# Weight slices of two output projections loaded one phase earlier, and small loads moved from ScalarE's queue to SyncE's

## What is computed

```python
for i in range(DEPTH_2):
    if i % N_MIXERS == 0:
        h, v_first = rwkv7_time_mix(...)      # ends in  y @ w_o
    else:
        h = dsa_attention(...)                # ends in  o @ w_o
    x = layer_norm(DN_ALPHA * x + h, ln_g[i, 0], ln_b[i, 0])
    f = conv_ffn(x, ffn_w_up[i], ffn_conv_w[i], ffn_conv_b[i], ffn_w_down[i])
    x = layer_norm(DN_ALPHA * x + f, ln_g[i, 1], ln_b[i, 1])
```

## Time and profile before

| | |
|---|---|
| median of 3 runs | 3757.14 us (3756.17 to 3758.62) |
| the profiled execution's own time | 3752.29 us |
| its span in the trace | 3750.5 us |
| busy in the span: PE, DVE, ACT, POOL | 94%, 61%, 40%, 36% |
| mean granted TensorE clock | 0.957 of full speed |
| scan phase | 2554 to 2606 us |
| first feed-forward phase begins | 2605.8 us |
| sparse attention | 3127 to 3298 us |
| SP issues the load of `sa_tb` | 3127.2 us |
| second feed-forward phase begins | 3297.9 us |

### The profile page before, as it was taken

How to read it: one execution, slowest core, us unless ns; L and a number is a source line. 1 busy time by engine, 2 the same in 40 slices (tenths; PEclk the granted TensorE clock), 3 DMA queues, 4 the chain that set the end, 5 groups by cost and what they waited for, 6 DMA issues and landing times. The chain is left out here.

```text
span 3750.5 us, 58365 instructions
## 1 busy us (share of the span) xinstructions
PE 3538.6 (94%) x22109; PEld 2871.8 (77%) x22109; DVE 2294.0 (61%) x3621; ACT 1483.8 (40%) x2442; POOL 1345.3 (36%) x822
## 2 busy tenths in 40 slices
PE   8999988998998999899999899898999998989998
PEld 4787866788988999788888343887888864677887
DVE  5713167416999887788888766445566236646642
ACT  3212255324445996333333243223255314424540
POOL 3724300424876334544222011330243521413352
PEclk9999988999999999999999999999899997699999
DMA  7634310625777899999999254203333331033331
GB/s 283 223 96 134 139 48 19 230 96 186 229 226 270 322 324 354 358 368 365 356 352 341 66 152 135 73 32 117 89 89 100 113 131 46 1 130 85 96 117 57
DMA packets 367108, 651.14 MB, mean 174 GB/s; under 512 B 23944, under 2 KB 227592, under 8 KB 363716
## 3 DMA queue, kind: packets, MB, share of 16 engines
q1 hardware_dynamic: 320028, 472.96, 38.0%
q0 software_dynamic: 36864, 134.23, 9.6%
q10 hardware_dynamic: 10024, 41.29, 2.8%
HBM read 557.64 MB, written 96.00 MB: 174 GB/s over the span
## 5 line engine op out<-in xcount | busy, mean ns | idle before, releaser
L97 PE MATMUL ex_hb<-wb_x_hi,ex_uh 128*128 128x384 f32 x1024 | 350.5, 342 | 22.7 <-POOL ex_ul L1677 22.7
L2404 POOL TENSOR_TENSOR pf_wl<-pf_raw,pf_wh 128x2048 fp32r<-128x2048 f32 x48 | 222.4, 4635 | 388.4 <-ACT pf_wh L2333 388.4
L98 PE MATMUL ex_hb<-wb_x_lo,ex_uh 128*128 128x384 f32 x1024 | 344.5, 336 | 0.0
L99 PE MATMUL ex_hb<-wb_x_hi,ex_ul 128*128 128x384 f32 x1024 | 344.3, 336 | 0.0
L97 PE MATMUL es_ob<-es_vh,es_ah 128*128 128x512 f32 x768 | 300.3, 391 | 10.7 <-DVE es_al L2046 10.7
L97 PE MATMUL pf_acc<-wb_x_hi,pf_wh 128*128 128x512 f32 (+2 forms) x768 | 298.2, 388 | 6.9 <-DVE wb_x_lo L2451 4.7
L98 PE MATMUL es_ob<-es_vl,es_ah 128*128 128x512 f32 x768 | 299.9, 391 | 0.0
L99 PE MATMUL es_ob<-es_vh,es_al 128*128 128x512 f32 x768 | 299.7, 390 | 0.0
L98 PE MATMUL pf_acc<-wb_x_lo,pf_wh 128*128 128x512 f32 (+2 forms) x768 | 297.6, 388 | 0.0
L99 PE MATMUL pf_acc<-wb_x_hi,pf_wl 128*128 128x512 f32 (+2 forms) x768 | 297.6, 387 | 0.0
L2025 POOL DMA_INDIRECT es_near<-in_peer_v,wb_picked x128 | 178.3, 1393 | 325.8 <-DVE wb_po L2049 319.7
(11 more groups left out here) (516 smaller groups left out, 8869.8 us busy)
## 6 DMA issues: line engine op xcount, KB each, us to landing
ex_u<-in_uT SPq DMA_DIRECT2D x128, 512.0 KB, 4.6
es_v<-in_peer_v SPq DMA_DIRECT2D x31, 2048.0 KB, 17.1
pf_raw<-in_w_up SPq DMA_DIRECT2D x88, 512.0 KB, 5.1
ip_raw<-in_w_in SPq DMA_DIRECT2D x112, 256.0 KB, 4.1
scratch_act<-ex_ge SPq DMA_DIRECT2D x128, 192.0 KB, 4.8
scratch_G<-eg_gates ACTq DMA_DIRECT2D x12, 2048.0 KB, 9.1
es_ge<-scratch_act SPq DMA_DIRECT2D x31, 768.0 KB, 6.0
es_g<-scratch_G SPq DMA_DIRECT2D x31, 768.0 KB, 10.0
```

The costliest lines, as they stand in the source:

```text
L97: pe.matmul(out, left[0], right[0], start=start, stop=False)
L98: pe.matmul(out, left[0], right[1], start=False, stop=False)
L99: return pe.matmul(out, left[1], right[0], start=False, stop=stop)
L2404: pool.tensor_tensor(wl[:, u], raw[:, u], wh[:, u].bitcast(F32), ALU.subtract).then_inc(w_lo, 1)
```

## The change

What it does:

- A new function `first_slices` allots the raw ring, `ph` and `pl` for each feed-forward phase ahead of the phase before it, with four semaphores of their own. To make room, `LATENT_AT` goes from 21944 to 17848, and the tiles that are carried into the RWKV phases are laid out in another order. The raw tile is now named `fo_raw` (first) and `fs_raw` (second), and so are `fo_ph`, `fo_pl`, `fs_ph`, `fs_pl`.
- In `rwkv_scan` SP issues the loads of slices 0 to 3 at the start. ACT makes the hi parts of slices 0 and 1 at the end of its rounds 4 and 5, DVE the lo parts in its rounds 5 and 6 (SPLIT = 2). SP then loads slices 4 and 5 into the two freed places.
- In `sparse_attention` SP issues the loads of slices 0 to 3 behind that of `sa_tb`. Nothing is split there (SPLIT = 0).
- In `projected_ffn` SP issues the five small loads first, then the slices that are left; ACT issues none. PE doesn't wait for the slices that were split ahead. The thresholds of the waits on `p_lo` go down by SPLIT.

```diff
+FIRST_RING = 4
+FIRST_SPLIT = 2
+def first_slices(nc, ctx, name, split):
+    with ExitStack() as own:
+        sb, _ = tensors(nc, own)
+        hold = sb(f"{name}_hold_a", [P, 18400])
+        pl = sb(f"{name}_pl", [P, KD, D], F32R)
+        hold = sb(f"{name}_hold_b", [P, 2520])
+        ph = sb(f"{name}_ph", [P, KD, D], F32R)
+        hold = sb(f"{name}_hold_c", [P, 3072])
+        raw = sb(f"{name}_raw", [P, 2, 2, D])
...
+def load_slice(sp, d_w, first, k):
+    ring = first[0][:].rearrange("p u s n -> p (u s) n")
+    sp.dma_start(ring[:, k % FIRST_RING], d_w.rearrange("(k p) n -> p k n", p=P)[:, k]).then_inc(first[3][k % FIRST_RING], 16)
...
 # projected_ffn, SP
-                for k in range(KD):
-                    if k >= RING:
-                        sp.wait_ge(p_lo, k - RING + 1)
+                sp.dma_start(ident[:], d["ident"]).then_inc(vec_loaded, 16)
+                sp.dma_start(gv[:], over_partitions(d["ln_g"][2 * n:2 * n + 1])).then_inc(vec_loaded, 16)
+                sp.dma_start(bv[:], over_partitions(d["ln_b"][2 * n:2 * n + 1])).then_inc(vec_loaded, 16)
+                sp.dma_start(cw[:], conv_w).then_inc(c_loaded, 16)
+                sp.dma_start(cb[:], conv_b).then_inc(c_loaded, 16)
+                for k in range(RING + SPLIT, KD):
+                    sp.wait_ge(p_lo, k - RING + 1 - SPLIT)
                     sp.dma_start(ring[:, k % RING], wp[:, k]).then_inc(p_loaded[k % RING], 16)
                 sp.dma_start(xr[:], d[x_in].rearrange("(t p) n -> p t n", p=P)).then_inc(rows_loaded, 16)
                 for u in range(2):
-                    sp.wait_ge(p_lo, KD - 2 + 2 * u)
+                    sp.wait_ge(p_lo, KD - 2 + 2 * u - SPLIT)
...
 # projected_ffn, PE
                 for k in range(KD):
-                    pe.wait_ge(p_lo, k + 1)
+                    if k >= SPLIT:
+                        pe.wait_ge(p_lo, k - SPLIT + 1)
                     project(0, k)
                     project(1, k)
...
 # projected_ffn, ACT (DVE's loop likewise: range(SPLIT, KD), p_hi, k - SPLIT + 1)
-                act.dma_start(ident[:], d["ident"]).then_inc(vec_loaded, 16)
-                act.dma_start(gv[:], over_partitions(d["ln_g"][2 * n:2 * n + 1])).then_inc(vec_loaded, 16)
-                act.dma_start(bv[:], over_partitions(d["ln_b"][2 * n:2 * n + 1])).then_inc(vec_loaded, 16)
-                act.dma_start(cw[:], conv_w).then_inc(c_loaded, 16)
-                act.dma_start(cb[:], conv_b).then_inc(c_loaded, 16)
-                for k in range(KD):
-                    act.wait_ge(p_loaded[k % RING], 16 * (k // RING + 1))
+                for k in range(SPLIT, KD):
+                    if k < RING + SPLIT:
+                        act.wait_ge(first_loaded[k % RING], 16 * (k // RING + 1))
+                    else:
+                        act.wait_ge(p_loaded[k % RING], 16)
                     act.activation(ph[:, k], ring[:, k % RING], ACT.Copy).then_inc(p_hi, 1)
...
 # rwkv_scan
+            @block.sync
+            def _(sp):
+                for k in range(FIRST_RING):
+                    load_slice(sp, d["w_o"], first, k)
+                for k in range(FIRST_SPLIT):
+                    sp.wait_ge(first_lo, k + 1)
+                    load_slice(sp, d["w_o"], first, FIRST_RING + k)
...
+                    if e in (4, 5):
+                        act.wait_ge(first_loaded[e - 4], 16)
+                        act.activation(ph[:, e - 4], ring[:, e - 4], ACT.Copy).then_inc(first_hi, 1)
...
+                    if e in (5, 6):
+                        dve.wait_ge(first_hi, e - 4)
+                        dve.tensor_tensor(pl[:, e - 5], ring[:, e - 5], ph[:, e - 5].bitcast(F32), ALU.subtract).then_inc(first_lo, 1)
...
 # sparse_attention, SP
                 sp.dma_start(tb[:], diagonals).then_inc(bias_loaded, 16)
+                for k in range(FIRST_RING):
+                    load_slice(sp, d["dsa_w_o"], first, k)
```

More of the change, by code:

```diff
@@ L2069, in _, with projected_ffn @@
                 dve.tensor_copy(xT[:, half, T - P:T], bank(TT - 1)[:, half]).then_inc(copied, 1)
-def projected_ffn(nc, d, x, w, n, x_in, x_out, onward=None, onward_loaded=None, bias_stored=None):
+FIRST_RING = 4
[9 more added lines that the diff above has]
+        raw = sb(f"{name}_raw", [P, 2, 2, D])
+    loaded = [ctx.enter_context(nc.semaphore(f"{name}_{i}_loaded", num=SLICES_BASE + (0 if split else FIRST_RING) + i)) for i in range(FIRST_RING)]
+    return raw, ph, pl, loaded, split
+def load_slice(sp, d_w, first, k):
+    ring = first[0][:].rearrange("p u s n -> p (u s) n")
+    sp.dma_start(ring[:, k % FIRST_RING], d_w.rearrange("(k p) n -> p k n", p=P)[:, k]).then_inc(first[3][k % FIRST_RING], 16)
+def projected_ffn(nc, d, x, w, n, x_in, x_out, first, onward=None, onward_loaded=None, bias_stored=None):
     ALPHA = 4.0 ** 0.25
@@ L3211, in _, with rwkv_scan @@
                         level_mask(n + 1, lv)
-def rwkv_scan(nc, d, gt, hs, pc, consts, r, y, split):
+def rwkv_scan(nc, d, gt, hs, pc, consts, r, y, split, first):
     HQ = KD // 2
@@ L3373, in _, with rwkv_recurrence @@
                                           ALU.subtract).then_inc(lo_done, 1)
-def rwkv_recurrence(nc, d, carried, stored, slot_loaded, masks_loaded, r, y, split):
+def rwkv_recurrence(nc, d, carried, stored, slot_loaded, masks_loaded, r, y, split, first):
     with ExitStack() as ctx:
@@ L3383, in rwkv_recurrence @@
         rwkv_chunks(nc, d, gt, hs, carried, stored, slot_loaded, masks_loaded, r, y)
[L3384 removed]
+        rwkv_scan(nc, d, gt, hs, carried[0], (carried[7], carried[9], carried[10]), r, y, split, first)
 AH = 16
@@ L3438, in _, with sparse_attention @@
                     dve.tensor_scalar(outs[n][1], op[:, n % 4, :], outs[n][2], None, ALU.mult).then_inc(dve_copied, 1)
-def sparse_attention(nc, d, o, split, bias_stored):
+def sparse_attention(nc, d, o, split, bias_stored, first):
     N = AH * TT
@@ L3652, in _, with sparse_block @@
                     act.activation(split[0][:, :, i * P:(i + 1) * P], rp[:, i % 2], ACT.Copy).then_inc(hi_done, 1)
-def sparse_block(nc, d, split, onward, loaded, bias_stored):
+def sparse_block(nc, d, split, onward, loaded, bias_stored, first):
     with ExitStack() as ctx:
@@ L3662, in sparse_block @@
         sparse_projections(nc, d, o, onward, loaded)
-        sparse_attention(nc, d, o, split, bias_stored)
+        sparse_attention(nc, d, o, split, bias_stored, first)
 def whole_block(nc, d):
```

47 lines of the change are left out of this document (29 added, 18 removed).

## The result

| | before | after |
|---|---|---|
| median, same chip | 3756.65 us (3752.62 to 3759.14) | 3740.89 us (3735.17 to 3744.6) |
| ratio | | 0.996, 95% interval 0.9949 to 0.9971 |
| the profiled execution's own time | 3752.29 us | 3744.6 us |
| its span | 3750.5 us | 3742.8 us |

The change is worth 15.8 us in the medians, 10.9 to 19.2 us by the interval. One of the changed kernel's six executions was disturbed and took 6393.03 us: the median counts it (without it, it is 3739.43), the range above and the ratio leave it out, and two experiments have one such execution each (4487.65 and 8706.19 us).

A forecast was written before the change was run, and what follows sets the result against it. PE was taken as the bound, busy 94% of the span, so gains come where it idles or runs slow. -5.8 - 4.05 - 1.5 - 6.05 + 0.3 = -17.1 us from 3757.14 gave median 3740.0, range 3732 to 3749.5.

The forecast's parts named there:

- First start, -5.8: First feed-forward phase: with slices 0 and 1 split ahead, PE's first matmul waits only for the barrier, -5.8 us.
- Second, -4.05: Second feed-forward phase: slices loaded but not split ahead, first matmul at 3300.35 instead of 3304.41, -4.05 us.
- Turns, -1.5 and -6.05: Turns of the normed rows: earlier feed-forward weights close PE's holes, -1.5 us in the first phase, -6.05 in the second.
- Rival A: Holes before the turns stay because weights come some 4 us later than estimated; only starts won, 3747.6; chance 0.18.
- The start of the projection: Projection's first matmuls: about 8 at the low clock, some 3.4 us, then the high clock.
- rival C: Clock stays at 1.2 GHz for most of each projection's first 22.4 us: +5.3, or 3769.8 with B's stretch; chance 0.03.
- Scan, +0.3: Scan: two added hi and two lo parts mostly hidden in waits, +0.3 us, bounds 0 and 1.2.
- Gate and table, 0 and 0: Slices' loads beside gate (scan) and `sa_tb` (sparse attention): cost 0 each, at most 1.3 and 2.3 us.
- The small loads, 0 by themselves: Five small loads moved from ACT to SP: cost nothing, give time only together with the slices loaded ahead.
- Rival B: Stretch at 1.2 GHz behind the fourth turn, 7.4 us: one more 3747.4, chance 0.12; one fewer 3732.6, chance 0.09.
- Rival D: Transfers ahead slow the phases before: gate 1.3, table 2.3, scan 1.2, giving 3744.5; counted within the forecast's 0.55.
- the 4.84 us: DVE's row at 2639.86, normally 1.29 us, takes 4.84 because DVE and POOL operations exclude each other for a whole instruction.

The follow-up runs named there:

- late-weights experiment: Changed kernel, with SP holding the first feed-forward weights back until PE is through with tiles 0 and 1: 3758.4 us in a single execution.
- the first phase alone: Kernel before, with only the first feed-forward phase getting its slices ahead, the second loading and splitting as before: 3742.91 us, ratio 0.9972.
- the second phase alone: Kernel before, with only the second feed-forward phase getting its slices ahead, the first as before: 3745.68 us, ratio 0.9975.
- the early turn alone: Kernel before, with only the fourth turn moved ahead of the last group of the first feed-forward product: 3734.95 us, ratio 0.9956.
- the run without splits: Changed kernel, slices 0 to 3 still loaded in the scan but none split, slices 4 and 5 not loaded there: 3741.83 us, ratio 0.9969.
- changed kernels with the early turn: Changed kernel with tile 3's turn one group of matmuls earlier, run twice: 3725.08 us, ratio 0.9916, and 3718.32 us, ratio 0.9911.
- the small loads alone: Kernel before, with only the five small loads moved from ACT to the head of SP's list: 3753.31 us, ratio 0.9999.

## Why the prediction was right

The median came out at 3740.89 against 3740.0. That they agree within 1 us is luck: the interval of the gain goes from 10.9 to 19.2 us, and the median without the longest execution is 3739.43. The steps are what can be judged:

- **First start, -5.8:** -5.81. **Second, -4.05:** -4.11. Taken from rows, and the rows held. PE was never starved for slices afterwards; the first awaited ones were there 8 to 9 us after the barrier, where I had allowed 13.
- **Turns, -1.5 and -6.05:** -1.09 and -5.94. The holes closed as forecast; the late-weights experiment opened them again. The times behind it were each off by 1 to 2 us and both later than I had them: POOL was done 29.5 us after the first matmul (2638.05 - 2608.55) and not 27.7, DVE came to `finish` after 29.2 and not 28.25. Rival A was nearer than I thought: tile 1's norm was ready at 2642.50 + 1.28 = 2643.8, 0.8 us ahead of the turns. There is a slip in my working too: the landing in the second phase is 3297.9 + 21.6 + 2 = 3321.5 by its own terms, not 3322.5; POOL was done 30.3 us after the first matmul there, I had 29.2. And the size of -6.05 hangs on the execution it was read from: in the run with the first phase alone the same unchanged stage took 73.23 and not 75.73 us, and against that the change gives 3.4 us.
- **The start of the projection:** this term I had as unchanged, 8 matmuls at the low clock. It was 13 in the first phase and about 11 in the second (busy stretch at 0.87 where the earlier trace rows had 0.93), some 5 x 0.195 = 1 us. This is rival C in a size of 1 us, not 11. It is more than the 0.4 us between -1.1 and -1.5, and it isn't a fixed cost: in the seven profiles whose first phase begins with two slices split, the clock rose 2.8 to 6.1 us after the first matmul; in the three with the old first start (the kernel before, the second phase alone, the early turn alone), 2.9 to 4.1 us.
- **Scan, +0.3:** 0.0. Behind the second lo part DVE came to the gate of the fourth chunk 0.9 us later than before, counted from the first row with x2, and two chunks later that was made up; the 1.3 us in the profiled pair lie ahead of the splits.
- **Gate and table, 0 and 0:** 0 and 0, but not alike. The gate was delayed by 5.3 of the 7.2 us of fullest sharing, and the margin covered it. The table was not delayed. Every profile in which both landings can be read says the same: the gate takes 19.7 or 19.8 us with the slices' loads beside it (four profiles) and 14.2 to 14.4 without (four); the table takes 13.1 to 13.8 us with the slices behind it (four) and 13.3 or 13.4 without (four). The gate comes from ACT's queue, the slices from SP's; the table and its slices share one queue. The Trainium skill (DMA: Bandwidth & Descriptors, "Queues, rings and completion order") says that a DMA engine goes round between the queue rows for which it has work, and the trace agrees; the sentence of the Trainium skill that I weighed in the prediction is about the queues of different engines; I had stretched it to two transfers in one queue, where these runs don't show it.
- **The small loads, 0 by themselves:** right for the total (0.9999). That they delay the starts by 4 us when the slices stand behind them, and that the stages would take back all but 1.3 us of it, I had not seen.
- **Rival B** is what the profiled pair shows: one more stretch, 7.4 us, so 7.7 instead of 15. I had it as an accident with a chance of 0.12. It is closer to a rule: behind a fourth turn with its wait, 16 of 18 phases in nine profiles ran the long stretch (34.7 to 36.4 us; the clock low for 20.5 to 23.9 of it), and none of six did without the wait (28.7 to 30.1; low for 3.4 to 6.8). The two exceptions are the first phase of the run without splits and the second phase of the profiled execution of before. So the sum was made against an execution that was fast in this place. That fits with its time being 4.85 us below the median shown, but the other executions were not profiled, and what share of them had the long stretch stays open.
- **Rival D,** the phases ahead pay: nothing is seen of it in the stages of the profiled pair. The gate's margin shrank to 1.9 us, and to 0.5 in another run; and in the two profiles of changed kernels with the early turn the scan's later part was 1 us longer, for a cause that stays open.

## What to carry to other kernels

A load moved ahead of a barrier gains what PE had waited for, if the next load in the chain moves too: start and next wait are coupled, as a later start (the small loads alone) and weights held back both showed. A short wait of PE, here 2.4 us, is dearer than it looks when a stretch at the low clock follows it, and here it was long where small matmuls came next; look at the granted clock behind each idle row, and fill the wait by issuing the small producer one group of matmuls earlier. A single profiled pair can hide half of a gain: read the difference by stages and ask of each stage whether the change touches it.

## What the runs showed of the hardware

- After 2.37 us without a matmul PE ran at 0.50 although it was busy for 12.00 of 12.00 us in the stretch that followed; the stage was 7.4 us longer than at the full clock. The Trainium skill (TensorE: Matmul & The Clock Gate, Part 1) says that the number of slow matmuls varies between runs; the traces agree, with 6 to 14 slow matmuls of 128x512 at the start of a projection.
- What PE did around the fall and the rise of the clock is the same in all 16 long cases: it fell at the beginning of the 96 matmuls of 128x128 (0.4 us ahead of the first to 2.7 us behind it) and rose 3.0 to 5.0 us after the first 128x512 behind them, 20.5 to 23.9 us in all. In the other eight phases (two with the wait, six with the early turn) the small matmuls ran at the high clock; there PE waited 2.2 us for POOL's third split, with matmuls of 128x512 next, and the clock was low for only 3.4 or 6.8 us. So two waits of nearly one length were followed by low stretches of very different lengths; in the rows they differ in what PE did next, and no run changes that alone, so why the clock stays low while PE is busy stays open. Taking the wait away took the long stretch away in 6 of 6 phases; why 2 of 18 escaped it with the wait was not found.
- A transfer of 4 MB was not delayed by 2 MB behind it in its queue (13.4 us both times), while 2 MB in ACT's queue took 19.7 us instead of 14.4 when 2 MB ran in SP's; the other profiles repeat both, as said above.
- DVE's operation `pf_x<-pf_x,pf_mv,pf_g` (1.28 us by itself) ended 1.08 us after POOL's subtraction in three cases where it had started before POOL's end: 2639.86 + 4.84 against 2643.62, 2637.73 + 1.40 against 2638.05, and 3324.17 + 2.45 against 3325.54. A fourth case shows both directions. In the second phase of before this operation (3332.72, 3.07 us) ended 1.09 us after POOL's first subtraction (3330.06 + 4.64), while POOL's second one took 5.60 us instead of 4.62; that is where the 10.17 us of the earlier trace rows come from, against 9.21 of the earlier trace rows. So each waits for the other's operation and then runs, as the prediction said of the 4.84 us.
